# The expert layer of prompt tiles 1 to 3 as a dense pass over all 16,384 experts, tile 0 and the sample gathered

## The chip, the core and the metric

The kernel runs on one core of a Trainium2 chip. The metric is the device time in microseconds (us); the median of three runs of the kernel before is 4337.53 us (4334.4 to 4338.32).

## What is computed

One decoder layer for 512 prompt tokens and a sample group of 8 × 8 tokens, all in fp32, with a model width of 2048: norm and input projection, two parallel mixers (latent attention and gated linear attention), output projection, then an expert layer, then an embedding gated by a sigmoid. The expert layer is what the change is about. Each token has 8 heads; a head picks 16 of 16,384 experts by product keys, and each expert is one row of `peer_u` and one of `peer_v`:

```python
top_s, sel = lax.top_k(cand, PEER_TOPK)
e = jnp.take_along_axis(cidx, sel, -1)
gate = jax.nn.softmax(top_s.astype(F32), -1)
act = jax.nn.gelu(jnp.einsum("td,thkd->thk", xb, w["peer_u"][e]), approximate=False)
coef = (gate * act).astype(xb.dtype)
return jnp.einsum("thk,thkd->td", coef, w["peer_v"][e])
```

An expert's number is e = i1 × 128 + i2, where i1 and i2 are the picks among two lists of 128 keys.

## The kernel before, in words

Tokens lie in tiles of 128: tiles 0 to 3 are the prompt, tile 4 (`PT`) the 64 sample tokens. The front of the layer runs over `GROUPS` [0], [1, 2], [3, 4]: norm, input projection (`project`, L826; for group 1 it runs ahead, L1288), attention and linear attention (`mixer`), output projection, norm, queries (L1251), key scores. An fp32 matrix product is a sum over 16 slices of 128 of the contraction; SP loads each slab of 1 MB into one of four slots `W`. Then `best_keys` and `route` on VectorE pick the experts and make `idx_all` and `gate_all`.

A tile has 8 units, one for a head (the sample's 64 tokens are doubled onto 128 partitions and take 4). A unit is 16 gathers of `peer_u` rows, each 128 × 2048, a dot product for each (`dot_products`, L1968), a Gelu on ScalarE (L2485), then 16 gathers of `peer_v` rows and 16 weighted adds into `total` (`weighted_sum`, L1993). GpSimd issues the indirect DMAs (`gathers`, L2549) into a ring of 8 slots. 36 units make 576 gathers of either kind.

The order is written by hand. The front's work on VectorE is a generator, `woven`, cut into steps at its `yield`s. The main loop runs through the gathered rows; after each, `row_taken` runs the steps whose entry in `ROWS_BEFORE` is at most the number of rows taken. `STEPS_BEFORE` does the same on ScalarE for each unit's Gelu, `PAGES_BEFORE` on GpSimd for the cache pages of the sample attention. Each engine's queue is in order, so a step that waits holds what stands behind it. PE's program has only the front and the embedding, in order: groups 0, 1, 2, then `PLE_GROUPS` [0, 1], [2, 3], [4] (`project` and `embed`, L848; the sample's by `sample_embedding`). Before an embedding pass, the summed rows come back through `h2_dram`. The columns of `z` leave by `z_rows` on ScalarE (L2115), into the buffer that held the key scores, so the second half of group 2's projection waits for `best_keys` (L1589).

## Time and profile before

| | us |
|---|---|
| median of the runs | 4337.53 |
| profiled execution, span | 4331.6 |
| PE (TensorE matmul) busy | 2254.9, 52% |
| DVE (VectorE) busy | 3288.1, 76% |
| ACT (ScalarE) busy | 522.0, 12% |
| POOL (GpSimd) busy | 2201.2, 51% |
| DMA | 1599.51 MB, mean 369 GB/s |

Busy time is what the engine spends in instructions; issuing a DMA and waiting are not counted, except that the indirect DMAs of GpSimd are. PEld is the loading of PE's weights and overlaps PE. The granted clock is a share of TensorE's full speed, so 1.00 is 2.4 GHz and 0.5 is 1.2 GHz. The name behind an arrow is what ended the idle time before an instruction.

### The profile page before, as it was taken

What the parts mean: (1) busy time and instruction counts of PE and PEld (TensorE: products, weight loads), DVE (VectorE), ACT (ScalarE), POOL (GpSimd) and SP (SyncE); (2) the same over time, 40 slices, a digit from 0 to 9 for tenths busy, and PEclk for the clock granted to TensorE, in tenths of its full rate; (3) what the DMA queues carried; (4) which work ended last, traced back from release to release, by engine and by line L of the source; (5) the groups of instructions that cost most, each with busy time, mean ns of one, the idle gap of its engine ahead of it and who ended that gap; (6) DMA issues with size and microseconds to landing.
All of it is one profiled execution on the core that took longest, in us unless ns stands there. A gap on an engine that the chain in (4) does not pass through costs nothing.

```text
span 4331.6 us, 24058 instructions
## 1 busy us (share of the span) xinstructions
PE 2254.9 (52%) x8238; PEld 1342.1 (31%) x8238; DVE 3288.1 (76%) x3700; ACT 522.0 (12%) x1098; POOL 2201.2 (51%) x1216
## 2 busy tenths in 40 slices
PE   8999815425899492779942457710000920000755
PEld 4456403213475131367731222710000410000322
DVE  0130699997667998868889856699999699988673
ACT  2220112122002001212212010000001000001001
POOL 0000365744332556468775653345667368877441
PEclk9999956657999796767865678955555965555877
DMA  8658789988997999989999899988989999999996
GB/s 294 250 223 287 303 357 364 422 323 335 424 423 299 422 424 414 353 356 365 406 374 360 347 400 413 405 345 339 399 365 405 424 415 422 422 407 422 424 408 234
DMA packets 261153, 1599.51 MB, mean 369 GB/s; under 512 B 27763, under 2 KB 49459, under 8 KB 91750
## 3 DMA queue, kind: packets, MB, share of 16 engines
q0 software_dynamic: 176064, 1268.30, 72.0%
q1 hardware_dynamic: 83078, 320.64, 19.5%
q10 hardware_dynamic: 1888, 9.03, 0.5%
q8 instruction: 65, 1.06, 0.1%
q14 instruction: 58, 0.48, 0.0%
HBM read 1554.75 MB, written 42.56 MB: 369 GB/s over the span
## 4 chain that ended last, share of the span: by engine, by line
PE 31%; DVE 30%; POOL 16%; DMA 13%; issue 7%; ACT 2%; SPq 0%; DVEq 0%; ACTq 0%; POOLq 0%
POOL ring L2549 16%; PE bank L826 14%; DVE ring L1968 11%; DVE total L1993 9%; DMA ring<-in_peer_v,idx_all 5%; DMA ring<-in_peer_u,idx_all 5%; PE bank L1251 4%; PE bank L1288 3%; PE bank L929 1%; PE bank L891 1%; PE bank L800 1%; PE bank L1079 1%; DMA front<-in_cache_kv_latent,page_rows 1%; DVE front L1744 1%; PE bank L1093 1%
## 5 line engine op out<-in xcount | busy, mean ns | idle before, releaser
L1993 DVE SCALAR_TENSOR_TENSOR total<-ring,gate_all,total 128x2048 f32<-128x2048 f32 x571 | 1341.8, 2350 | 188.0 <-DMA ring<-in_peer_v,idx_all 164.5
L2549 POOL DMA_INDIRECT ring<-in_peer_u,idx_all x576 | 1062.2, 1844 | 795.7 <-DVE total L1993 359.1
L2549 POOL DMA_INDIRECT ring<-in_peer_v,idx_all x576 | 1072.2, 1861 | 711.9 <-DVE total L1993 376.3
L1968 DVE CUSTOM_DVE_ANT_0 ring<-ring,xrow 128x2048 f32<-128x2048 f32 x576 | 1297.5, 2287 | 169.4 <-DMA ring<-in_peer_u,idx_all 167.5
L826 PE MATMUL bank<-front 128*128 128x512 f32 (+3 forms) x1920 | 838.3, 594 | 68.9 <-ACT front L2115 64.6
L800 PE MATMUL bank<-inv_diag,front 128*128 128x128 f32 (+1 forms) x304 | 61.9, 391 | 1159.3 <-DVE inv_diag L1378 1102.2
L826 PEld LDWEIGHTS bank<-front 128*128 128x128 f32 (+1 forms) x1920 | 338.4, 181 | 558.5 <-issue 554.5
L800 PEld LDWEIGHTS bank<-inv_diag,front 128*128 128x128 f32 (+1 forms) x304 | 58.9, 299 | 1164.2 <-DVE inv_diag L1378 1098.2
L1251 PE MATMUL bank<-front 128*128 128x128 f32 (+2 forms) x1536 | 257.0, 329 | 20.5 <-DMA front<-in_peer_w_q 17.4
L1251 PEld LDWEIGHTS bank<-front 128*128 128x128 f32 x1536 | 239.8, 192 | 39.3 <-DMA front<-in_peer_w_q 20.3
L2574 POOL DMA_DIRECT2D ring<-in_w_in x12 | 10.7, 894 | 342.8 <-PE bank L1288 239.6
L1373 DVE RECIPROCAL st<-st 128x1 f32<-128x1 f32 (+1 forms) x20 | 3.2, 161 | 225.8 <-ACT st L2049 225.8
L1288 PE MATMUL bank<-ring 128*128 128x490 f32 x384 | 163.8, 574 | 2.1 <-ACT front L2115 2.1
L2485 ACT ACTIVATE dots<-dots 128x16 f32<-128x16 f32 x36 | 7.7, 215 | 804.2 <-DVE dots L1968 759.3
L913 PE MATMUL bank<-ident,front 128*128 128x128 f32 (+1 forms) x20 | 4.6, 380 | 170.9 <-DVE front L1426 99.4
L1288 PEld LDWEIGHTS bank<-ring 128*128 128x128 f32 x384 | 70.4, 190 | 74.7 <-issue 71.6
L1196 PE MATMUL bank<-front 128*128 128x128 f32 (+1 forms) x288 | 41.7, 314 | 93.0 <-DVE front L1695 81.9
L2501 POOL DMA_DIRECT2D xrow<-xn_dram x6 | 3.4, 573 | 163.1 <-DMA z_dram<-total 102.7
L1079 PE MATMUL bank<-ident,front 128*128 128x128 f32 x256 | 74.8, 395 | 7.4 <-DMA front<-in_cache_kv_latent,page_rows 5.8
L1575 DVE MAX8 front<-front 128x8 f32<-128x128 f32 (+1 forms) x80 | 19.2, 281 | 76.4 <-ACT front L2325 75.5
L1415 DVE TENSOR_TENSOR g_mla<-g_mla 128x128 f32<-128x128 f32 x1 | 0.3, 291 | 100.3 <-DMA g_mla<-in_qk_gain_q 100.3
L1119 PE MATMUL bank<-front 128*64 128x256 f32 x256 | 70.5, 444 | 6.9 <-ACT front L2357 6.9
(323 smaller groups left out, 2894.0 us busy)
## 6 DMA issues: line engine op xcount, KB each, us to landing
front<-in_w_in SPq DMA_DIRECT2D x64, 980.0 KB, 8.4
front<-in_w_out SPq DMA_DIRECT2D x48, 1024.0 KB, 9.1
front<-in_peer_w_q SPq DMA_DIRECT2D x48, 1024.0 KB, 13.3
front<-in_w_ple_gate SPq DMA_DIRECT2D x48, 1024.0 KB, 9.1
ring<-in_w_in POOLq DMA_DIRECT2D x12, 1960.0 KB, 10.5
front<-in_w_uq SPq DMA_DIRECT2D x6, 1536.0 KB, 10.7
ring<-in_peer_u,idx_all POOLq DMA_INDIRECT x576, 14.3
ring<-in_peer_v,idx_all POOLq DMA_INDIRECT x576, 16.0
```

The costliest lines, as they stand in the source:

```text
L800: mm = e.matmul(out, row, inv_diag[:R, :R], start=True, stop=True)
L826: mm = e.matmul(bank[4 * sl + c][:R, 0:ncol], XT[:, k, sl * P:sl * P + R], W[:, n % SLABS, c * ncol:(c + 1) * ncol], start=(k == 0), stop= ...
L891: mm = e.matmul(bank[c][:R, :], XT[:, k, 0:R], W[:, n % SLABS, c * BANK:(c + 1) * BANK], start=(k == 0), stop=False)
L929: mm = e.matmul(bank[j][:R, 0:2 * QK], cqT[:, slot(t), k, 0:R], wq[:, k, j * 2 * QK:(j + 1) * 2 * QK], start=(k == 0), stop=(k == 3))
L1079: e.transpose(bank[k][:, j * P:(j + 1) * P], latb[:, i, k * P:(k + 1) * P], ident[:, :])
L1093: mm = e.matmul(S, lt[0:ROPE, 2, j * P:(j + 1) * P], qrT[0:ROPE, b, :], start=False, stop=True)
L1119: e.matmul(bank[7][0:NS, 0:KVR], pTs[:, pg, :], latb[:, pg % HALF, :], start=(pg == 0), stop=False)
L1251: mm = e.matmul(bank[j][:, 0:ntok], W[:, n % SLABS, at:at + P], XT[:, k, 0:ntok], start=(k == 0), stop=(k == KD - 1))
L1288: mm = e.matmul(bank[6 + sl][:, 0:IN_BANK], xt[:, k, sl * P:(sl + 1) * P], chunk(n)[:, k % 8, :], start=(k == 0), stop=(k == KD - 1))
L1968: e.tensor_tensor_reduce(out=ring[:, b, :], in0=ring[:, b, :], in1=xrow[:, t % 2, :], scale=1.0, scalar=0.0, op0=ALU.mult, op1=ALU.add, ac ...
L1993: e.scalar_tensor_tensor(out=total, in0=ring[:, b, :], scalar=c1, in1=total, op0=ALU.mult, op1=ALU.add).then_inc(s("summed"), 1)
L2549: e.indirect_dma_start(out=ring[:, k % RING, :], out_offset=None, in_=a[("peer_u", "peer_v")[side]][0], in_offset=bass.IndirectOffsetOnAxi ...
```

## The change

Only tile 0 (8 units) and the sample (4 units) still gather. For tiles 1 to 3, 384 tokens (`ND`), every expert is computed:

- Two inputs are laid out anew on the host: `peer_u_t`, 128 tiles of 128 experts with the contraction on partitions, and `peer_v_t`, 32 blocks of 4 expert tiles, cut in four quarters of 512 columns.
- `route` keeps i1, i2 and the gate of each of a token's 128 picks in `picks` instead of making indices. `spread` turns them on PE (`picksT`), makes two one-hot matrices for each token on VectorE (128 picks × 128 keys, one of them times the gate), multiplies them on PE, which gives the 128 × 128 gates of the token, and stores these in `g_dram` through ScalarE's copies and DMA queue, 16 tokens at a time.
- PE turns the normed rows of the three tiles into `XD` (`turn_rows`). For each of 32 blocks (`NBLOCKS`) `expert_scores` makes 4 × 16 products of 384 columns, ScalarE applies Gelu into `CT`, VectorE multiplies by the block's gates (`weigh`), `expert_sums` makes 48 products of 512 columns (4 quarters × 3 tiles × 4 expert tiles) in 4 banks, and VectorE adds each of 12 sums to `acc` (`add_sums`). SP loads each megabyte into one of 5 buffers, two of them until the routes are done, and the block's gates in runs of 64 numbers.
- PE's order is now: groups 0 and 1, the projections of group 2, spreads 0 and 1, the mixer of group 2, `turn_rows`, scores of blocks 0 and 1, spread 2, then sums of b and scores of b + 2 in turn, then the embedding of all tiles in the groups [0], [1, 2], [3, 4].
- The ring has 5 slots. The three order tables are new: `STEPS_BEFORE` has 12 entries instead of 36, `ROWS_BEFORE` 1,207 instead of 705, with a last value of 384 gathered rows instead of 1,124. `h2_dram` and `sample_embedding` are gone; the embedding reads `h_dram` and adds `acc`. Some semaphores are shared.

The diff, cut to its core, without the tables:

```diff
-UNITS = PH * PT + PH // 2
-FIRST_UNITS = [t * PH for t in range(T)] + [UNITS]
+GATHERED, DENSE = [0, PT], [1, 2, 3]
+UNITS = PH + PH // 2
+FIRST_UNITS = {0: 0, PT: PH}
+UNITS_OF = {0: range(PH), PT: range(PH, UNITS)}
+XR = {0: 0, PT: 1}
 LAST = len(GROUPS) - 1
+ND = P * len(DENSE)
+ETILES = NKEY
+EB = 4
+NBLOCKS = ETILES // EB
+TURNS = 4 * len(DENSE)
+UNITS_V = 4 * len(DENSE)
+D_BUFS = 5
+FEW = 2
+FEW_LOADS = len(DENSE) + 3 * EB
+DENSE_LOADS = len(DENSE) + 2 * ETILES
+GROUP = 4
+CHUNK = 16
+G_GROUPS = P // GROUP
+G_CHUNKS = ND // CHUNK
+V_BANKS = [2, 3, 6, 7]
+LAST_DENSE = DENSE[-1]
...
+RING_SLOTS, RING = 8, 5
+STAGE = 6
+TILE_OF = [t for t in GATHERED for _ in UNITS_OF[t]]
...
+        XD = carve(KD, ND, at=0)
+        CT = [carve(EB, ND), carve(EB, ND)]
+        d_first = carve(D)
+        GB = [carve(G_CHUNKS, EB * CHUNK, at=h0 - 2 * EB * P), carve(G_CHUNKS, EB * CHUNK)]
+        d_bufs = [d_first, ring[:, RING, :]] + [carve(D, at=h0 + D), carve(D), carve(D)]
+        acc = [ring[:, STAGE, :], ring[:, STAGE + 1, :], carve(D, at=y0 + 2 * D + 4 * PLE)]
+        stage = [ring[:, STAGE + i, :].rearrange("p (i n) -> p i n", n=CHUNK) for i in range(2)]
+        onehot = xrow[:, XR[PT], :].rearrange("p (b w n k) -> p b w n k", b=2, w=2, n=GROUP)
...
+            def turned_rows():
+                e.wait_ge(s("xn_stored"), 16 * T)
+                e.wait_ge(s("slabs_used"), PASSES["gate0"])
+                for i, t in enumerate(DENSE):
+                    n = load_of("x", 0, i)
+                    d_free(e, n)
+                    e.dma_start(d_bufs[d_buf(n)], xn_dram[rows(t), :]).then_inc(d_sem(n), 16)
+            def expert_columns(b):
+                for i in range(EB):
+                    n = load_of("u", b, i)
+                    d_free(e, n)
+                    e.dma_start(d_bufs[d_buf(n)], a["peer_u_t"][EB * b + i]).then_inc(d_sem(n), 16)
+            def expert_rows(b):
+                for i in range(EB):
+                    n = load_of("v", b, i)
+                    d_free(e, n)
+                    if n >= FEW_LOADS:
+                        e.wait_ge(s("route_ready"), len(ROUTES))
+                    e.dma_start(d_bufs[d_buf(n)], a["peer_v_t"][b, i]).then_inc(d_sem(n), 16)
+            def gates(b):
+                if b >= 2:
+                    e.wait_ge(s("c_ready"), b - 1)
+                else:
+                    e.wait_ge(s("topk_done"), PH * (LAST_DENSE + 1))
+                    for i in range(2):
+                        e.wait_ge(s(f"g_stored{i}"), 16 * G_CHUNKS // 2)
+                e.dma_start(GB[b % 2], g_dram[:, :, EB * b:EB * (b + 1), :].rearrange("c p i n -> p c (i n)"))\
+                    .then_inc(s(f"pair_landed{b % 2}"), 16)
...
+            turned_rows()
+            expert_columns(0)
+            expert_columns(1)
...
+            for b in range(NBLOCKS):
+                gates(b)
+                if b >= 2:
+                    expert_columns(b)
+                if b >= 1:
+                    expert_rows(b - 1)
+            expert_rows(NBLOCKS - 1)
...
+            def spread(j):
+                e.wait_ge(s("picks_ready"), j + 1)
+                for w in range(3):
+                    mm = e.transpose(bank[7][:, w * P:(w + 1) * P], picks[:, w, :], ident[:, :])
+                mm.then_inc(s("picksT_psum"), 1)
+                for q in range(G_GROUPS):
+                    n = j * G_GROUPS + q
+                    e.wait_ge(s("onehot_ready"), n + 1)
+                    if n >= 2:
+                        e.wait_ge(s("g_staged"), n - 1)
+                    for i in range(GROUP):
+                        mm = e.matmul(bank[4 + n % 2][:, i * P:(i + 1) * P], onehot[:, n % 2, 1, i, :], onehot[:, n % 2, 0, i, :],
+                                      start=True, stop=True)
+                    mm.then_inc(s("g_psum"), 1)
+                    yield
+                e.wait_ge(s("g_staged"), (j + 1) * G_GROUPS)
+            def turn_rows():
+                e.wait_ge(s("scores_sb"), 4 * T)
+                for i in range(len(DENSE)):
+                    n = load_of("x", 0, i)
+                    e.wait_ge(d_sem(n), d_landed(n))
+                    for q in range(4):
+                        m = 4 * i + q
+                        if m >= 2:
+                            e.wait_ge(s("dense_sb"), m - 1)
+                        for j in range(4):
+                            k = 4 * q + j
+                            mm = e.transpose(bank[m % 2][:, j * P:(j + 1) * P], d_bufs[d_buf(n)][:, k * P:(k + 1) * P], ident[:, :])
+                        mm.then_inc(s("dense_psum"), 1)
+            def expert_scores(b):
+                for i in range(EB):
+                    n, m = load_of("u", b, i), TURNS + EB * b + i
+                    e.wait_ge(d_sem(n), d_landed(n))
+                    e.wait_ge(s("dense_sb"), max(m - 1, TURNS))
+                    for k in range(KD):
+                        mm = e.matmul(bank[m % 2][:, 0:ND], d_bufs[d_buf(n)][:, k * P:(k + 1) * P], XD[:, k, :],
+                                      start=(k == 0), stop=(k == KD - 1))
+                    mm.then_inc(s("dense_psum"), 1)
+            def expert_sums(b):
+                e.wait_ge(s("c_ready"), b + 1)
                 for c in range(4):
...
+                    n = load_of("v", b, c)
+                    e.wait_ge(d_sem(n), d_landed(n))
+                    for sl in range(len(DENSE)):
+                        u = UNITS_V * b + len(DENSE) * c + sl
+                        if u >= len(V_BANKS):
+                            e.wait_ge(s("v_added"), u - len(V_BANKS) + 1)
+                        for i in range(EB):
+                            mm = e.matmul(bank[V_BANKS[u % len(V_BANKS)]][:, :], CT[b % 2][:, i, sl * P:(sl + 1) * P],
+                                          d_bufs[d_buf(n)][:, i * BANK:(i + 1) * BANK], start=(i == 0), stop=(i == EB - 1))
+                        mm.then_inc(s("v_psum"), 1)
...
+                if g == LAST:
+                    for j in range(len(DENSE) - 1):
+                        now(spread(j))
...
+            turn_rows()
+            expert_scores(0)
+            expert_scores(1)
+            now(spread(len(DENSE) - 1))
+            for b in range(NBLOCKS):
+                expert_sums(b)
+                if b + 2 < NBLOCKS:
+                    expert_scores(b + 2)
...
+                if t in DENSE:
+                    if DENSE.index(t):
+                        e.wait_ge(s("picksT_psum"), DENSE.index(t))
+                    mark(e.tensor_copy(picks[:, 0, :], e1))
+                    mark(e.tensor_copy(picks[:, 1, :], e2))
+                    link(e.tensor_tensor(picks[:, 2, :].rearrange("p (h k) -> p h k", h=nh), g3,
+                                         gsum[:, 0:nh].unsqueeze(2).to_broadcast([P, nh, TOPK]), ALU.mult))
+                    e.sem_inc(s("picks_ready"), 1)
+                    e.sem_inc(s("route_ready"), 1)
+                    yield
+                    return
...
+            def spread(j):
+                yield
+                e.wait_ge(s("picksT_sb"), j + 1)
+                for q in range(G_GROUPS):
+                    n = j * G_GROUPS + q
+                    yield
+                    if n >= 2:
+                        e.wait_ge(s("g_psum"), n - 1)
+                    for i in range(GROUP):
+                        t = GROUP * q + i
+                        e.tensor_scalar(onehot[:, n % 2, 0, i, :], iota[:, :], picksT[:, 0, t:t + 1], picksT[:, 2, t:t + 1],
+                                        ALU.is_equal, ALU.mult)
+                        ins = e.tensor_scalar(onehot[:, n % 2, 1, i, :], iota[:, :], picksT[:, 1, t:t + 1], None, ALU.is_equal)
+                    ins.then_inc(s("onehot_ready"), 1)
+                yield
+            def weigh(b):
+                yield
+                e.wait_ge(s("dense_sb"), TURNS + EB * (b + 1))
+                e.wait_ge(s(f"pair_landed{b % 2}"), 16 * (H_GLA // 2 + b // 2 + 1))
+                ct = CT[b % 2].rearrange("p i (c n) -> p i c n", n=CHUNK)
+                e.tensor_tensor(ct, ct, GB[b % 2].rearrange("p c (i n) -> p i c n", i=EB), ALU.mult).then_inc(s("c_ready"), 1)
+            def add_sums(b):
+                for u in range(UNITS_V):
+                    n = UNITS_V * b + u
+                    yield
+                    e.wait_ge(s("v_psum"), n + 1)
+                    to = acc[u % len(DENSE)][:, u // len(DENSE) * BANK:(u // len(DENSE) + 1) * BANK]
+                    turned = bank[V_BANKS[n % len(V_BANKS)]][:, :]
+                    if b == 0:
+                        e.tensor_copy(to, turned).then_inc(s("v_added"), 1)
+                    else:
+                        e.tensor_tensor(to, to, turned, ALU.add).then_inc(s("v_added"), 1)
+            def experts():
+                yield from weigh(0)
+                for b in range(NBLOCKS):
+                    if b + 1 < NBLOCKS:
+                        yield from weigh(b + 1)
+                    yield from add_sums(b)
+                yield
...
+                    if t in DENSE:
+                        i = DENSE.index(t)
+                        e.wait_ge(s("rows_loaded"), ROWS_IN["ffn", LAST] + 16 * sum(x in DENSE for g in PLE_GROUPS[:pg + 1] for x in g))
+                        e.wait_ge(s("v_added"), UNITS_V * NBLOCKS + i)
+                        e.tensor_tensor(H[:, sl, :], H[:, sl, :], acc[i], ALU.add).then_inc(s("v_added"), 1)
...
+                yield from mixer(1)
+                yield from first_route(1)
+                yield from other_routes(1)
+                yield from spread(0)
+                yield from spread(1)
+                yield from mixer(2)
+                yield from best_keys(PT - 1, 0, PH)
+                yield from route(PT - 1, 0, PH)
+                yield from spread(2)
+                yield from best_keys(PT, 0, PH)
+                yield from route(PT, 0, PH)
+                yield from experts()
+                for pg in range(len(PLE_GROUPS)):
                     yield from embedding(pg)
             e.memset(eps[:, :], EPS).then_inc(s("fills_ready"), 1)
...
+                e.copy(picksT[:, :, :].rearrange("p w n -> p (w n)"), bank[7][:, 0:3 * P]).then_inc(s("picksT_sb"), 1)
+                per = CHUNK // GROUP
+                for q in range(G_GROUPS):
+                    n = j * G_GROUPS + q
+                    c, at = n // per, n % per * GROUP
+                    yield
+                    e.wait_ge(s("g_psum"), n + 1)
+                    if at == 0 and c >= 2:
+                        e.wait_ge(s(f"g_stored{c % 2}"), 16 * (c // 2))
+                    e.copy(stage[c % 2][:, :, at:at + GROUP].rearrange("p i n -> p n i"),
+                           bank[4 + n % 2][:, :].rearrange("p (n i) -> p n i", n=GROUP)).then_inc(s("g_staged"), 1)
+                    if at == CHUNK - GROUP:
+                        e.wait_ge(s("g_staged"), n + 1)
+                        e.dma_start(g_dram[c], stage[c % 2]).then_inc(s(f"g_stored{c % 2}"), 16)
+                yield
...
+                    e.activation(CT[b % 2][:, i, :], bank[m % 2][:, 0:ND], ACT.Gelu).then_inc(s("dense_sb"), 1)
...
+    u = np.ascontiguousarray(np.asarray(inputs["peer_u"], np.float32)[0].reshape(NKEY, NKEY, KD, P).transpose(0, 3, 2, 1)).reshape(NKEY, P, D)
+    v = np.ascontiguousarray(np.asarray(inputs["peer_v"], np.float32)[0].reshape(NBLOCKS, EB, P, 4, BANK).transpose(0, 3, 2, 1, 4))\
+        .reshape(NBLOCKS, 4, P, EB * BANK)
+    for name, v in (("peer_u_t", u), ("peer_v_t", v)):
+        arrays[f"in_{name}"] = v
+        a[name] = nc.dram_tensor(f"in_{name}", v.shape, F32, kind="ExternalInput").ap()
```

## Rows read from the trace of the kernel before

**Rows 1.** The page, part 2: the span in 40 slices, busy tenths and granted clock.

```profile
PE   8999815425899492779942457710000920000755
...
DVE  0130699997667998868889856699999699988673
...
PEclk9999956657999796767865678955555965555877
```

**Rows 2.** The page, part 5: the two gather groups.

```profile
L1993 DVE SCALAR_TENSOR_TENSOR total<-ring,gate_all,total 128x2048 f32<-128x2048 f32 x571 | 1341.8, 2350 | 188.0 <-DMA ring<-in_peer_v,idx_all 164.5
...
L1968 DVE CUSTOM_DVE_ANT_0 ring<-ring,xrow 128x2048 f32<-128x2048 f32 x576 | 1297.5, 2287 | 169.4 <-DMA ring<-in_peer_u,idx_all 167.5
```

**Rows 3.** Windows: length, busy us (x) of PE, PEld, DVE, ACT, POOL; clock, DMA share, GB/s.

```profile
0.00:579.00 579.00, 504.86 (x1839) 284.22 (x1839) 166.73 (x420) 102.99 (x236) 65.67 (x53) 0.96 0.74 269
579.00:1040.00 461.00, 163.37 (x594) 107.08 (x594) 431.15 (x461) 94.61 (x180) 286.29 (x146) 0.62 0.90 364
1040.00:1325.00 285.00, 254.36 (x928) 171.83 (x928) 185.32 (x150) 39.78 (x90) 89.24 (x67) 0.94 0.99 410
1325.00:1662.00 337.00, 238.85 (x576) 92.72 (x576) 299.23 (x563) 29.10 (x72) 159.30 (x93) 0.84 0.96 394
1662.00:2537.00 875.00, 503.12 (x2451) 371.48 (x2451) 742.72 (x736) 153.30 (x282) 591.24 (x289) 0.66 0.93 371
2537.00:2831.00 294.00, 236.07 (x926) 148.29 (x927) 194.30 (x143) 30.38 (x82) 120.27 (x80) 0.91 1.00 409
2831.00:4332.00 1501.00, 354.23 (x927) 166.42 (x924) 1268.68 (x1233) 71.88 (x159) 889.14 (x489) 0.61 0.95 387
```

**Rows 4.** Windows, L1968 alone: the two mixing stages.

```profile
579.00:1040.00 461.00, 168.28 (x150) 0.62 0.90 364
...
1662.00:2537.00 875.00, 287.44 (x256) 0.66 0.93 371
```

**Rows 5.** Windows, L1993 alone: the same two stages.

```profile
579.00:1040.00 461.00, 159.80 (x69) 0.62 0.90 364
...
1662.00:2537.00 875.00, 312.12 (x133) 0.66 0.93 371
```

**Rows 6.** Timeline of PE, 84 to 175: start, length, line, shape, count.

```profile
84.99 52.88 PE L826 MATMUL bank<-front 128*128 128x490 f32 x128 [0.75 <-ACT front L2115]
...
163.83 5.32 PE L929 MATMUL bank<-front 128*128 128x384 f32 x16
```

**Rows 7.** A window in which PE is busy throughout, columns as in rows 3.

```profile
300.00:470.00 170.00, 169.21 (x831) 111.42 (x829) 19.32 (x72) 21.05 (x56) 0.88 (x1) 1.00 0.78 276
```

**Rows 8.** Timeline of ACT, 1420 to 1665: the wait between the two projections.

```profile
1522.21 1.98 ACT L2115 COPY front<-bank 128x490 f32<-128x490 f32 x4 [96.75 <-DVE front L1589]
```

**Rows 9.** Groups of DVE by form: count, busy, mean ns.

```profile
L1902 DVE TENSOR_TENSOR front<-front,bank 128x512 f32<-128x512 f32 x16 | 10.9, 680 | 3.7 <-PE bank L848 3.7
L1854 DVE TENSOR_TENSOR front<-front,iota 128x1536 f32<-128x1536 f32 x6 | 10.5, 1754 | 0.1
...
L1484 DVE TENSOR_SCALAR ms<-ms 128x1 f32<-128x1 f32 x32 | 4.9, 154 | 1.1
...
L1378 DVE TENSOR_SCALAR inv_diag<-ident,st 128x128 f32<-128x128 f32 x12 | 3.6, 298 | 0.4
```

**Rows 10.** DMA issues: count, KB each, median us to landing.

```profile
front<-in_w_out SPq DMA_DIRECT2D x48, 1024.0 KB, 9.1
...
front<-in_state_gla SPq DMA_DIRECT2D x4, 1024.0 KB, 21.4
```

**Rows 11.** Timeline of PE, the last two-tile embedding pass.

```profile
4036.75 110.14 PE L826 MATMUL bank<-front 128*128 128x512 f32 x256 [0.46 <-ACT front L2394]
4147.66 13.97 PE L848 MATMUL bank<-front 128*128 128x512 f32 x32 [0.78 <-ACT front L2417]
```

**Rows 12.** Timeline of SP around the same pass: its store, the next pass's first load.

```profile
4168.91 5.64 SPq L763 DMA_DIRECT2D out_y_p<-front  x2
4182.98 0.50 SPq L758 DMA_DIRECT2D front<-in_p_sample  x1
```

413 lines of the change are left out of this document (203 added, 210 removed), and 85 rows, old and new, of the table ROWS_BEFORE.

## The prediction

> **What bounds the kernel now.** I read the span in slices first [rows 1]. VectorE (DVE) is at 6 to 9 tenths from slice 5 on, while TensorE (PE) is full only in the first slices and in blocks later and is nearly silent in slices 28 and 29 and 33 to 36, at the lower of its two clocks (5 tenths, 1.2 GHz). Then the costliest groups [rows 2]: the two gather operations, one dot product and one weighted add per gathered expert row, hold DVE for 1297.5 + 1341.8 = 2639 of its 3288 us. Then the stages [rows 3]: after 2831 us PE has 354 us of work in 1501 us while DVE has 1269 us; up to there the mixer stages run at a clock of 0.62 (579 to 1040) and 0.66 (1662 to 2537), with gaps. So the end is set by a queue of 1,152 gather operations of 2.3 us, woven into the mixer's DVE work. PE has room, but how much decides this case: busy time times granted clock, summed over the seven windows, is 505×0.96 + 163×0.62 + 254×0.94 + 239×0.84 + 503×0.66 + 236×0.91 + 354×0.61 = 1789 us of PE at full clock, and the idle parts pull those clocks down, so it is at least that.
>
> **The price of one matmul.** The code's second input projection has 16 steps of 4 matmuls, 64 calls; the timeline shows 128 rows in 52.88 us [rows 6], so every fp32 matmul is two rows, and a call of 490 columns costs 0.826 us. One row of 384 columns starts each 5.15/16 = 0.322 us (the next line starts at 168.98 us; 5.32 us less the overlap of the last), so a call costs 0.644 us; 512 columns take 110.14/256 = 0.430 us a row, 0.860 a call [rows 6, 11]. The clock in such stretches is 1.00, 2.4 GHz [rows 7].
>
> **Added: the dense pass on PE.** Scores: 128 expert tiles × 16 calls of 384 columns, 10.3 us a tile. Sums: 32 blocks × 4 quarters × 3 token tiles × 4 calls of 512, 12 × 0.860 = 10.3 us a quarter. A block is 8 × 10.3 = 82.5 us, 32 of them 2640 us, all in one engine's queue and nothing beside it on PE. PE's floor rises to 1789 + 2640 = 4430 us, above the present span of 4331.6 us, before any gap is counted.
> What feeds it is light. Per block: 8 loads of 1 MB (9.1 us each to landing, [rows 10]), five buffers, one consumed in 10.3 us; the gates, 3,072 runs of 256 B. The nearest row for short runs is the state load, 1,024 runs of 1 KB in 21.4 us [rows 10]; three times that is 64 us, still under 82.5 us and double-buffered. DVE: one product of 1,536 elements, 1.75 us, 12 adds of 512 at 0.68 us, 8.2 us, and 5.3 of the sample's gathered rows, 12 us: 22 us of 82.5 [rows 9]. ScalarE (ACT): 4 Gelus of 384 columns, under 3 us. So I take 82.5 us; the upper end is 86 (a gap at each hand-over), the lower end 82.
> The page "DMA: Bandwidth & Descriptors", section Specifications, of the Trainium skill speaks against the gate loads: transfers under 512 B are below line rate. No row here shows 256 B runs by themselves; even at a tenth of line rate the 0.79 MB would take about 20 us as an estimate, and the sum stays as it is.
>
> **Added: the dense gates.** Three spreads of 32 groups. A group is 8 one-hot operations of 128 columns on DVE, 4 calls on PE, one copy on ACT, a DMA issue on ACT's queue every fourth. For the one-hot operation there is only the neighbour L1378, 298 ns alone, and 154 ns for one column [rows 9]; back to back I take 0.20 us, 1.6 us a group plus hand-over, 55 us a spread (bounds 40 and 85). Spreads 0 and 1 stand in PE's program between the projections and the mixer of the last group, so the mixer waits for both: +110 us. Spread 2 is below.
>
> **Removed: 24 of 36 gather units**, 768 gathered rows: 768 × 2.32 = 1782 us of DVE, 805 MB. Only part was on the path before 2831 us. I counted the weaving steps of each stage in the code and looked them up in the new table: mixer of group 1 now has 60 gather rows beside it (table 16 to 76), the last mixer 95 (140 to 235), and the sample's 128 rows fall in dense blocks 0 to 22. What falls away:
> - 0 to 579: five rows fewer, −11, so 568.
> - 579 to 1040, 461 us: rows now cost 168 + 160 = 328 us [rows 4, 5]; DVE's other work is 103 us, so the rest is dependency latency. 60 rows are 137 us. A row taken away gives back between 0 and its whole length; I take 0.6 (PE's clock and gaps say that the chain is about half of it): 461 − 0.6 × 191 = 346. End 914.
> - 1040 to 1325, 285 us, PE 254 busy: stays. End 1199.
> - 1325 to 1662: the second projection waited for the selection, 96.75 us of ACT's wait [rows 8], because gather rows and selection shared DVE. Without them the two projections run on: 22 + 105 + 3 + 105 + 2 = 237, then spreads 0 and 1, 110 + 5. End 1551 against 1662; the gain of the selection is eaten by the spreads.
> - 1662 to 2537, 875 us, rows 287 + 312 = 600 us, now 217: 875 − 0.6 × 383 = 645. End 2196 against 2537.
> - 2537 to 2831, 294 us: fewer DMA waits, 270. End 2466.
>
> **Moved: start of the dense pass.** PE reloads and turns the rows of tiles 1 to 3 (25 us, three loads moved to SP's queue), does scores of blocks 0 and 1 with only two buffers (83 us), then spread 2 (55 us). DVE then selects for the sample tile, 57 us (114 us of non-gather work for two tiles, 1325 to 1662 [rows 3 to 5] less the gathers), and takes its first gathered row, about 28 us with the spread and load of the row on SP's and POOL's queues, before it weighs block 0. First sums at 2466 + 25 + 83 + 4 + 55 + 60 + 28 = 2721. PE idles some 85 us of that. The rest is 32 sum halves and 30 score halves: 62 × 41.25 = 2557. End 5278.
>
> **Moved: the embedding.** All five tiles now follow the last add, where before most lay under gathers. A two-tile pass is 110 + 14 us of PE [rows 11], about 35 us of loads, squares and transposes ahead and 14 us of store behind (4168.91 to 4182.98, [rows 12], the wait of the next pass for the store): 171. The one-tile pass: 14 + 57 + 8 + 13 = 92. Together 92 + 171 + 170 = 433. End 5711; the four stores of the summed rows go. The medians lie 6 us above the profiled execution's 4331.6, so 5717, rounded to 5720.
>
> **Rivals.**
> A. The gathers were the whole of the mixer stages (a row gives back 1.0): −76 and −153 us, 5490. For it: DVE 431 of 461 busy [rows 3]. Against it: PE and ACT chains at half clock in between.
> B. They were none of it (0), or the woven order, fixed for other durations, makes PE wait: DVE waits for a gathered row inside the adds, ACT for dot products ahead of a Gelu, four banks buffer only 10 us. With 0 the time is +115 +230 = 6060; 10 us in 23 blocks are +230, 5950. For it: ACT waits for dots in queue order; against it: DVE has 60 us of 82.5 free.
> C. The other side, not slower: a matmul is streamed once where I count twice. The place is the dense pass, the price 41 us a block; 5720 − 1320 = 4400, and with A's −229 it is 4171, faster. It decides once a block is under about 39 us alone, or 46 with A. Against it: 64 calls in 52.88 us [rows 6].
> The page "FP8 and Floating Point Precision", section TensorE Precision Notes, of the Trainium skill gives true fp32 four passes through the array; by that rule, 512 columns at 2.4 GHz take 0.853 us, and the trace's 0.860 agrees.
> D. The pass doesn't stay at 2.4 GHz for 2.6 ms. The longest stretch that the trace has is some 470 us at 1.00 [rows 1, 7]; beyond it nothing is shown. If a tenth of the clock goes, +290, 6010.
>
> **How the numbers follow.** Forecast 0.68, A 0.10, B 0.12, C 0.01, D 0.05, the rest spread about. The forecast's own bounds: gather share 0.6 ± 0.25 is ∓145, spreads −45 to +90, blocks −15 to +110, tail ± 30; together about −150 and +160. The range reaches a little to A and B: 5540 to 5910. About 0.2% is what a measurement of this kernel can tell from no change. Faster 0.01 (C), within 0.2% 0.01, slower 0.98: this rests on the floor of 4430 us, not on the weaving.
>
> **What would show it.** The changed profile should have PE at 9 tenths with clock 1.00 in nearly half of the slices; 4,096 score rows of 384 columns and 3,072 sum rows of 512 at 0.32 and 0.43 us; a block every 82.5 us; DVE under 4 tenths there, DMA under 5. The last mixer's norm should come near 2196, the first sum near 2721, the last near 5278. Gaps of PE within blocks with a releaser on DVE or ACT would be B; mixer stages of 270 and 490 us A. A block of 41 us would prove the forecast wrong as a whole.

## The result, and the profile after

| | before | after |
|---|---|---|
| median, us | 4337.92 | 5759.47 (5752.01 to 5768.67) |
| ratio to before | | 1.328, 95% interval 1.326 to 1.330 |
| profiled execution, span, us | 4331.6 | 5764.9 |
| PE busy | 52% | 87% |
| DVE busy | 76% | 35% |
| DMA, MB | 1599.5 | 1105.6 |

The change makes the kernel 1421.6 us slower. Of the page of the changed kernel, these are the busy times, four lines of the 40 slices (PE, DVE, granted clock, DMA), the chain by engine, and the largest groups of the dense sums (L1063) and dense scores (L1048); those that read a buffer in `ring` stand in smaller groups of their own.

```profile
PE 5022.0 (87%) x16199; PEld 2808.4 (49%) x16199; DVE 2027.1 (35%) x3672; ACT 651.6 (11%) x1283; POOL 570.6 (10%) x438
...
PE   8996546889668965895699999999999999999789
...
DVE  0306676462873456336322222322232211111110
...
PEclk9998668999876776998899999999999999999999
DMA  8586658854455448642655555555555533332543
...
PE 82%; DVE 10%; DMA 3%; ACT 2%; issue 2%; SPq 0%; POOL 0%; DVEq 0%; ACTq 0%
...
L1063 PE MATMUL bank<-front 128*128 128x512 f32 x2424 | 1047.6, 592 | 0.0
L1048 PE MATMUL bank<-front 128*128 128x384 f32 x3200 | 1041.3, 487 | 5.0 <-DMA front<-in_peer_u_t 5.0
```

PE is at 9 tenths in all slices from 20 to 36 (counted from 0), with the clock at 9; before, PE was nearly silent in much of that half [rows 1]. DVE is at 1 to 3 tenths beneath it. 82% of the chain is PE. The windows by stage (length, busy us of PE, PEld, DVE, ACT, POOL with counts, clock, DMA share, GB/s) are group 1's mixer, spreads 0 and 1, the last mixer, its output and queries, the start of the dense pass, the dense pass, and the embedding:

```profile
573.00:918.00 345.00, 165.00 (x594) 108.69 (x594) 242.68 (x329) 90.41 (x176) 100.56 (x61) 0.64 0.62 231
1454.00:1603.00 149.00, 83.67 (x519) 71.59 (x519) 137.08 (x528) 73.41 (x82) 13.88 (x8) 0.87 0.52 202
1603.00:2277.00 674.00, 501.02 (x2451) 371.04 (x2452) 366.89 (x484) 138.40 (x265) 169.09 (x119) 0.71 0.57 211
2277.00:2535.00 258.00, 235.87 (x944) 150.60 (x944) 65.42 (x79) 31.42 (x85) 19.41 (x18) 0.94 0.64 241
2535.00:2786.00 251.00, 130.94 (x547) 87.17 (x547) 168.56 (x649) 46.46 (x55) 8.11 (x8) 0.80 0.32 112
2786.00:5352.00 2566.00, 2560.65 (x6912) 1314.68 (x6912) 599.64 (x607) 61.07 (x125) 127.11 (x124) 1.00 0.48 161
5352.00:5765.00 413.00, 350.36 (x891) 157.07 (x890) 41.65 (x56) 52.07 (x126) 0.00 (x0) 0.92 0.44 158
```

These answer to [rows 3]. The front of the layer ends at 2535 us instead of 2831, 296 us earlier, although the spreads take 145 us of it. Behind it stood 1501 us; now it is 3230, and 2566 of them are the sixth row, in which PE is idle for 5 us, at a clock of 1.00.

### The profile page after: what moved, and what is told of

Same layout as the page of the kernel before. It is cut to its first block, busy times and chain, and to the rows that moved or that the text cites. A ratio compares the mean times of both kernels' runs of the same rounds, so it can differ in the third digit from the quotient of the medians.

```text
span 5764.9 us, 39836 instructions
## 1 busy us (share of the span) xinstructions
PE 5022.0 (87%) x16199; PEld 2808.4 (49%) x16199; DVE 2027.1 (35%) x3672; ACT 651.6 (11%) x1283; POOL 570.6 (10%) x438
## 4 chain that ended last, share of the span: by engine, by line
PE 82%; DVE 10%; DMA 3%; ACT 2%; issue 2%; SPq 0%; POOL 0%; DVEq 0%; ACTq 0%
PE bank L1063 23%; PE bank L1048 23%; PE bank L979 16%; PE bank L1414 4%; PE bank L1451 3%; DVE xrow L2079 2%; DVE xrow L2081 1%; PE bank L953 1%; PE bank L1282 1%; PE bank L1092 1%; PE bank L1256 1%; PE bank L1242 1%; DVE total L2244 1%; PE bank L1254 1%; DVE ring L2219 1%
## 5 line engine op out<-in xcount | busy, mean ns | idle before, releaser
L1063 PE MATMUL bank<-front 128*128 128x512 f32 x2424 | 1047.6, 592 | 0.0
L1048 PE MATMUL bank<-front 128*128 128x384 f32 x3200 | 1041.3, 487 | 5.0 <-DMA front<-in_peer_u_t 5.0
L1048 PEld LDWEIGHTS bank<-front 128*128 128x128 f32 x3200 | 608.7, 190 | 435.3 <-issue 12.5
L1063 PEld LDWEIGHTS bank<-front 128*128 128x128 f32 x2424 | 460.6, 190 | 574.6 <-issue 568.0
L2244 DVE SCALAR_TENSOR_TENSOR total<-ring,gate_all,total 128x2048 f32<-128x2048 f32 x190 | 446.4, 2350 | 80.9 <-DMA ring<-in_peer_v,idx_all 77.9
L2219 DVE CUSTOM_DVE_ANT_0 ring<-ring,xrow 128x2048 f32<-128x2048 f32 x192 | 436.7, 2286 | 96.4 <-DMA ring<-in_peer_u,idx_all 95.6
L2825 POOL DMA_INDIRECT ring<-in_peer_v,idx_all x192 | 259.6, 1352 | 1688.3 <-DVE total L2244 1237.9
L2825 POOL DMA_INDIRECT ring<-in_peer_u,idx_all x192 | 262.2, 1366 | 1362.2 <-DVE dots L2219 1094.0
L1063 PE MATMUL bank<-ring,front 128*128 128x512 f32 x648 | 284.5, 595 | 90.7 <-DMA ring<-in_peer_v_t 90.7
L1048 PE MATMUL bank<-front,ring 128*128 128x384 f32 x896 | 297.6, 491 | 5.5 <-ACT front L2663 4.8
L1414 PEld LDWEIGHTS bank<-front 128*128 128x128 f32 x1536 | 240.6, 192 | 18.4 <-issue 3.6
L1063 PEld LDWEIGHTS bank<-ring,front 128*128 128x128 f32 x648 | 123.8, 191 | 245.2 <-issue 243.6
L1048 PEld LDWEIGHTS bank<-front,ring 128*128 128x128 f32 x896 | 172.0, 192 | 128.0 <-issue 13.1
```

Source lines behind the costliest of these rows:

```text
L1048: mm = e.matmul(bank[m % 2][:, 0:ND], d_bufs[d_buf(n)][:, k * P:(k + 1) * P], XD[:, k, :], start=(k == 0), stop=(k == KD - 1))
L1063: mm = e.matmul(bank[V_BANKS[u % len(V_BANKS)]][:, :], CT[b % 2][:, i, sl * P:(sl + 1) * P], d_bufs[d_buf(n)][:, i * BANK:(i + 1) * BANK], ...
L1414: mm = e.matmul(bank[j][:, 0:ntok], W[:, n % SLABS, at:at + P], XT[:, k, 0:ntok], start=(k == 0), stop=(k == KD - 1))
L2219: e.tensor_tensor_reduce(out=ring[:, b, :], in0=ring[:, b, :], in1=xrow[:, XR[t], :], scale=1.0, scalar=0.0, op0=ALU.mult, op1=ALU.add, ac ...
L2244: e.scalar_tensor_tensor(out=total, in0=ring[:, b, :], scalar=c1, in1=total, op0=ALU.mult, op1=ALU.add).then_inc(s("summed"), 1)
L2825: e.indirect_dma_start(out=ring[:, n % RING, :], out_offset=None, in_=a[("peer_u", "peer_v")[side]][0], in_offset=bass.IndirectOffsetOnAxi ...
```

## What was expected and what came

The ends of the changed kernel's stages beside the predicted ones, in us; the last column is the miss of that stage alone:

| end of | predicted | measured | miss of the stage |
|---|---|---|---|
| first stage | 568 | 573.5 | +5.5 |
| mixer of group 1 | 914 | 918.3 | −1 |
| output, queries of group 1 | 1199 | 1200 | −3 |
| projections of group 2 | 1436 | 1457.8 | +21 |
| spreads 0 and 1 | 1551 | 1603.0 | +30 |
| last mixer | 2196 | 2277.0 | +29 |
| its output and queries | 2466 | 2535 | −12 |
| start of the sums | 2721 | 2786.4 | −4 |
| last sum | 5278 | 5352 | +9 |
| last store | 5711 | 5765 | −20 |

## Experiments

A time without an interval is that of a single run. A kernel's line numbers can lie a few above those of the changed kernel.

**1. Half of the dense products.**

```diff
-                    for k in range(KD):
-                        mm = e.matmul(bank[m % 2][:, 0:ND], ...
+                    for k in range(KD // 2):
+                        mm = e.matmul(bank[m % 2][:, 0:ND], ...
...
-                        for i in range(EB):
+                        for i in range(EB // 2):
                             mm = e.matmul(bank[V_BANKS[u % len(V_BANKS)]][:, :], ...
```

> Leaves out half of the dense products: a score sums 8 of its 16 slices of the contraction, a sum takes 2 of its 4 expert tiles; loads, gates, Gelus, weighing and adds stay. Theory (the count of PE's matmul rows at 2.4 GHz sets the dense pass, everything else has room): a block falls from 82.5 to 41.3 us, so the 2566 us from the first sum to the last become about 1283 and the time 5759 - 1283 = 4476 us. Rival (the feed is the next limit): the same 427 MB must come in 1283 us, 333 GB/s as a mean and about 356 in the blocks with gathered rows, against 161 now; if they come at 300 GB/s, blocks take 48 us and the time is about 4650. Rival of the adds: VectorE needs 22 us of a block and would not show.

Measured: 4469.4 us. Windows of it, in the blocks with gathered rows, and from the first sum to the last:

```profile
2840.00:3340.00 500.00, 500.00 (x1362) 258.36 (x1361) 257.31 (x260) 24.70 (x52) 66.74 (x67) 1.00 0.98 364
2753.00:4062.00 1309.00, 1290.35 (x3472) 662.53 (x3473) 578.22 (x610) 65.74 (x133) 128.65 (x124) 0.99 0.88 316
```

The dense pass took 1309 us for the expected 1283; the difference lies in its first 87 us, where two loads came 14 us late and the clock was at 0.88. PE has no idle time in the first of these windows although DMA is at 0.98 of its time and moves 364 GB/s. So the count of matmul rows sets the pass, and halving the rows halves it: 5759.5 − 4469.4 = 1290 us for 16 of 32 blocks' worth, 40.3 us a half block. Even at this half price, with half of the products left out, the single run is 3% slower than the kernel before.

**2. A quarter of the feed.**

```diff
-                    e.dma_start(d_bufs[d_buf(n)], a["peer_u_t"][EB * b + i]).then_inc(d_sem(n), 16)
+                    e.dma_start(d_bufs[d_buf(n)][:, 0:D // 4], a["peer_u_t"][EB * b + i][:, 0:D // 4]).then_inc(d_sem(n), 16)
```

and the same for `peer_v_t`.

> Leaves out three quarters of each load of an expert tile (512 of 2048 columns are loaded; the products run over old numbers). Theory (loads are fully hidden behind PE): the dense pass keeps 2566 us; only the first sum comes a few us earlier; 5745 to 5765 us. Rival (loads slow PE's or VectorE's access, or end small waits at hand-overs): 1 us a block or more, 5730 or less.

Measured: 5754.0 us, ratio to before 1.326 (1.324 to 1.329), not to be told from the changed kernel's. A window of its dense pass, columns as above:

```profile
2786.00:5338.00 2552.00, 2548.38 (x6889) 1309.46 (x6888) 596.15 (x605) 61.19 (x125) 127.45 (x124) 1.00 0.28 85
```

85 GB/s instead of 161, and PE as busy as before; from the first sum to the last it takes 2563.5 us instead of 2565.2. Three quarters of the loads, with whatever contention they bring, are worth nothing in the fp32 pass. The hand-overs between engines stay in this run; what they can cost is bounded by PE's 5 us of idle time in the changed kernel. Together with experiment 1 this closes the dense pass: its price is its matmul rows.

**3 and 4. What tile 0's gathered rows cost the mixers.** First only their work on DVE, then the gathers altogether.

```diff
+                    w = P if t == 0 else D
-                    e.tensor_tensor_reduce(out=ring[:, b, :], in0=ring[:, b, :], in1=xrow[:, XR[t], :], ...
+                    e.tensor_tensor_reduce(out=ring[:, b, 0:w], in0=ring[:, b, 0:w], in1=xrow[:, XR[t], 0:w], ...
```

> Leaves out 15 of 16 columns of tile 0's dot products and weighted adds on VectorE (128 of 2048); its gathers and all waits stay. It asks what a gathered row costs a mixer stage. Theory (by parts of the stage: where PE is at 9 tenths, as in the sample attention, a row costs 0.15 of its length; in the linear attention 0.87; in the latent attention 0.3): the last mixer has 224 us of such work and falls from 704 by about 80 to some 625 us; the mixer of group 1 (136 us of such work) from 345 to about 275; the time is about 5605. Rival (0.6 everywhere, as predicted): 704 - 117 = 587, 5570. Rival (whole): 704 - 195 = 509, 5446. Rival (nothing): 5759. The dense pass keeps 2566 us in all of them.

```diff
+                    if t in SKIP:
+                        e.memset(dots[:, XR[t], i:i + 1], 0.5).then_inc(s("dots_done"), 1)
+                        row_taken()
+                        continue
```

with `SKIP` = [0], the same for the weighted adds, and no indirect DMA for these rows.

> Leaves out the gathers of tile 0 altogether: no indirect DMA, and each dot product and weighted add of tile 0 is one fill of a single column, with the same order of steps. The run with thin rows fell by 59 us only, because VectorE then waited 369 us for the rows' DMAs instead. Theory (by parts of the stage; a removed row gives back 0.15 in the sample attention, where PE is at 9 tenths, 0.3 in the latent attention, 0.87 in the linear attention, all of it in the tail): the last mixer falls from 704 to about 610, that of group 1 from 345 to about 275; with 25 us at the spreads, where six gathered adds are left, the time is about 5575. Rival (what is left of the mixers is their own chain of dependent steps and hides rows of tile 0 wholly): last mixer 660 as with thin rows, 5700. Rival (0.6 everywhere): 570 and 263, 5525.

Measured: 5700.8 us with thin rows, where 5605 was expected, and 5625.9 us with none, where 5575 was. The expectations took the last mixer from the wrong point: 704 us counts the last 30 us of the spreads in; it is 674, from PE's first transpose at 1603.0 (below) to the norm at 2277.0. By that measure it falls to 634 with thin rows (1575.9 to 2210.4) and to 627 with none (1509.8 to 2136.8); group 1's mixer from 345 to 337 and 280; the spreads from 135 to 122 and 120 us, first matmul to last. The two gather groups of DVE in the mixers and spreads, first in the changed kernel (573 to 2277 us):

```profile
L2219 DVE CUSTOM_DVE_ANT_0 ring<-ring,xrow 128x2048 f32<-128x2048 f32 x112 | 254.6, 2287 | 59.9 <-DMA ring<-in_peer_u,idx_all 59.3 <-DVE front L1914 0.4 <-DVE front L1723 0.2
L2244 DVE SCALAR_TENSOR_TENSOR total<-ring,gate_all,total 128x2048 f32<-128x2048 f32 x106 | 249.3, 2352 | 45.5 <-DMA ring<-in_peer_v,idx_all 42.9 <-DVE front L1723 0.2
```

then in the thin one (573 to 2211 us):

```profile
L2246 DVE SCALAR_TENSOR_TENSOR total<-ring,gate_all,total 128x128 f32<-128x128 f32 x106 | 37.1, 350 | 107.4 <-DMA ring<-in_peer_v,idx_all 105.3 <-DVE front L1723 0.2
L2220 DVE CUSTOM_DVE_ANT_0 ring<-ring,xrow 128x128 f32<-128x128 f32 x112 | 30.7, 286 | 132.6 <-DMA ring<-in_peer_u,idx_all 132.0 <-DVE front L1914 0.4 <-DVE front L1723 0.2
```

DVE's work on these rows has fallen from 504 to 68 us, but the wait for the rows to land (the number after the second bar) has grown from 105 us to 240. Only 59 us of the kernel's time came back with the work; another 75 came back when the gathers went too. So a gathered row in DVE's in-order queue is priced by its landing as well as by the operation on it. The expectation missed this: all three theories priced only DVE's work.

With the rows gone the prices by part come out. Three parts of the last mixer, latent attention, sample attention and linear attention, first before (columns as above):

```profile
1662.00:1868.00 206.00, 97.32 (x301) 50.36 (x301) 192.30 (x199) 41.82 (x81) 133.31 (x67) 0.64 0.95 376
1934.00:2224.00 290.00, 262.56 (x1517) 208.43 (x1517) 251.63 (x214) 52.62 (x102) 235.42 (x111) 0.78 0.93 377
2224.00:2486.00 262.00, 81.23 (x332) 57.38 (x330) 237.34 (x278) 38.88 (x65) 162.65 (x77) 0.60 0.94 367
```

then in the changed kernel:

```profile
1603.00:1751.00 148.00, 95.34 (x301) 48.18 (x301) 98.71 (x140) 37.63 (x77) 42.39 (x31) 0.71 0.64 237
1821.00:2090.00 269.00, 260.72 (x1516) 207.95 (x1516) 112.59 (x120) 50.22 (x98) 61.73 (x48) 0.80 0.49 179
2090.00:2240.00 150.00, 77.83 (x333) 55.14 (x331) 108.58 (x187) 33.22 (x59) 37.80 (x22) 0.67 0.60 212
```

and without tile 0's rows:

```profile
1510.00:1638.00 128.00, 92.13 (x301) 46.12 (x300) 39.24 (x126) 37.58 (x77) 4.80 (x5) 0.74 0.22 80
1704.00:1972.00 268.00, 261.39 (x1513) 207.99 (x1513) 44.48 (x103) 50.22 (x98) 14.98 (x16) 0.79 0.16 58
1972.00:2118.00 146.00, 80.25 (x334) 57.67 (x334) 59.62 (x169) 33.20 (x59) 0.56 (x1) 0.67 0.27 87
```

| part | before: gather work, length | after | no rows |
|---|---|---|---|
| latent attention | 157, 206.0 | 62, 148.1 | 0, 128.3 |
| its preparation for the sample | 30, 66.3 | 14, 70.2 | 0, 66.0 |
| sample attention | 213, 289.2 | 71, 268.4 | 0, 267.8 |
| linear attention | 179, 262.1 | 50, 149.9 | 0, 146.0 |
| tail | 21, 51.4 | 22, 37.4 | 0, 18.9 |
| sum | 600, 875 | 219, 674 | 0, 627 |

The lengths are read between PE's first instructions of each part (the tail begins with PE's last matmul of the linear attention), the gather work from L1968 and L1993 (L2219 and L2244 after) alone. In the sample attention PE is busy 263 of 290 us before and 261 of 268 without any row: it is bound by PE, and 213 us of gather work cost it 21. In the linear attention PE works only 81 of 262 us; there the first 129 us of removed work gave back 112, the last 50 gave back 4. So the share is no property of a row: it was 0.87 where DVE had hardly any idle time (linear attention, DVE busy 237 of 262 us) and 0.15 where PE had hardly any (sample attention, 21 of 142 us). It also falls as rows go, and the name of the busiest engine doesn't tell it: after the change DVE is still the busiest one of the linear attention (109 of 150 us, PE 78), yet its last 50 us gave back 4, while the 22 us of the tail, in which PE has nothing to do, gave back 18.5. The predicted 0.6 was right for group 1's mixer (345 us, predicted 346), whose remaining 136 us of rows then gave back 65, and a little high for the last mixer (201 of 381 us removed, 0.53), as a mean over parts as different as these.

**5. The sums' earlier start.**

```diff
                 yield from spread(2)
+                yield from weigh(0)
+                yield from weigh(1)
+                yield from add_sums(0)
                 yield from best_keys(PT, 0, PH)
```

with `gates`, `expert_rows(0)` and `expert_columns(2)` ahead of the sample's spread on SP, and `expert_gelus(2)` ahead of the route on ACT.

> The same computation. After spread 2 VectorE weighs blocks 0 and 1 and adds the sums of block 0 before it selects for the sample tile (tile 3's part waits in the buffer total, since its own place is still used by the selection), SP loads the gates and the rows of block 0 and the columns of block 2 ahead of the sample's spread, ScalarE does the Gelus of block 2 first. Theory (PE's 91 us of idle time before the first sum are the selection of the sample, its spread and first gathered row, all of which can lie beside sums of block 0 and scores of block 2): what stays is the load of the gates, some 25 to 35 us; 5759 - 60 = about 5700 us. Rival (the gates of block 0, in runs of 256 B, land late, some 60 us after the last spread): the gain is 20 us or less, 5740. Rival (the selection moves on and PE waits for it later, before the sums of block 1): 5750.

Measured: 5732.7 us (1.321, 1.319 to 1.323), 27 us less, not 60. In the changed kernel PE's timeline has one wait here:

```profile
2786.39 12.47 PE L1063 MATMUL bank<-ring,front 128*128 128x512 f32 x24 [90.66 <-DMA ring<-in_peer_v_t]
```

In this one it has three (first sum, then sums of block 1):

```profile
2699.04 6.53 PE L1066 MATMUL bank<-ring,front 128*128 128x512 f32 x8 [17.07 <-DMA ring<-in_peer_v_t]
...
2821.44 11.95 PE L1066 MATMUL bank<-front 128*128 128x512 f32 x24 [36.81 <-issue]
...
2851.10 9.05 PE L1066 MATMUL bank<-ring,front 128*128 128x512 f32 x16 [14.28 <-DVE ring L2109]
```

The gates were quicker than expected: 17 us from the last spread to the first sum, where 25 to 35 were named. But the selection of the sample now stands behind block 0's adds, and by SP's program the loads of `peer_v_t` for block 1 come after its end (36.8 us of PE; the row names no releaser); then DVE takes the sample's first dot products, which wait for their rows (15.3 us for the first), before it weighs and adds again (14.3 us of PE). The three waits together are 68 of the 91 us: the rival was right that the wait moves on, the theory that part of it is gone.

**6. The kernel before without the gathers of tiles 1 to 3.** The edit is that of experiment 4 with `SKIP` = [1, 2, 3].

> The kernel before, without the gathers of tiles 1 to 3 (no indirect DMA, each dot product and weighted add a fill of a single column) and without the dense pass: it leaves out the expert layer of these tiles. It asks what the gathers of the three tiles were worth on the path, 1782 us of VectorE's work. Theory (stages as in the changed kernel, without its spreads: ends at 573, 918, 1200, 1454, 2158, 2416; then 114 us of selection for two tiles, 28 to the first gathered row, 128 rows of 2.33 us, 90 us of the last embedding): about 2950 us, so the gathers held 1390 us of the path, 0.78 of their work. Rival (the gathers were the whole of it): 4338 - 1782 = 2556. Rival (half of them lay in gaps): 3450.

Measured: 3274.8 us. Windows of group 1's mixer, of the last mixer, its output and queries, and of the rest:

```profile
580.00:1043.00 463.00, 167.23 (x594) 108.84 (x594) 430.90 (x461) 94.83 (x180) 280.99 (x145) 0.61 0.90 363
1602.00:2231.00 629.00, 488.83 (x2452) 364.88 (x2453) 164.78 (x611) 153.84 (x282) 24.29 (x27) 0.74 0.23 82
2231.00:2487.00 256.00, 232.91 (x928) 147.98 (x928) 14.16 (x127) 30.98 (x83) 0.00 (x0) 0.93 0.45 146
2487.00:3273.00 786.00, 355.81 (x922) 166.06 (x922) 458.12 (x1039) 71.43 (x158) 229.31 (x137) 0.72 0.67 265
```

The theory had 2950. So the three tiles' gathers held 4338.9 − 3274.8 = 1064 us of the path, 0.60 of their 1782 us. The theory missed by 325 us, at three places above all. Group 1's mixer stays at 463 us (345 expected), since all of its rows are tile 0's: in the changed kernel it got shorter only because the new table puts fewer of them there. The last mixer takes 629 us (704 expected, in which the end of the spreads was counted), as it does without tile 0's rows above, so 628 is its own length. And the rest takes 786 us instead of 530: the table, made for other durations, puts the embedding's steps, in which DVE waits 121 us for PE's products of one pass, between the sample's rows. So 1064 us is the price of the gathers with this order of steps left as it was; an order made for the kernel without them could only make it larger. Against the same kernel the dense way to these three tiles costs 5759.5 − 3274.8 = 2485 us; the matmuls alone are 2640 us of PE in it.

**7 and 8. One row per matmul.** ScalarE rounds every loaded megabyte to bf16.

```diff
+                    e.wait_ge(d_sem(m), d_landed(m))
+                    if m - H_BUFS >= len(DENSE):
+                        used_by_pe(e, m - H_BUFS)
+                    e.copy(h_bufs[m % H_BUFS], d_bufs[d_buf(m)]).then_inc(s("keysT_sb"), 1)
...
-                        mm = e.matmul(bank[m % 2][:, 0:ND], d_bufs[d_buf(n)][:, k * P:(k + 1) * P], XD[:, k, :],
+                        mm = e.matmul(bank[m % 2][:, 0:ND], h_bufs[n % H_BUFS][:, k * P:(k + 1) * P], XD[:, k, :],
```

`XD` and `CT` are bf16 too, and `keysT_sb`, a semaphore that was free by then, counts the rounded loads.

> Changes the arithmetic of the dense pass: ScalarE rounds each loaded megabyte, the turned rows and the Gelus to bf16, the gate product is bf16, and the sums are fp32 in the banks; everything else stays fp32. Theory (each matmul is then one row at 1 column a cycle, so PE needs 64 x 0.16 + 48 x 0.215 = 20.6 us a block, a quarter of 82.5, and the feed becomes the bound: 9.2 MB a block, with the gathered rows of blocks 0 to 22 some 14.9 MB, at the 420 GB/s that the trace shows at best, 36 and 22 us a block): the dense pass takes about 1020 us instead of 2566, the time is about 4210 us. Rival (ScalarE, with eight copies of 1.9 us and its turns with PE in one queue, or VectorE's adds, add up instead of overlapping): 45 us a block, 4630. Rival (bf16 matmuls cost as much as fp32's): 5760.

> The bf16 arithmetic of the dense pass as in the other kernel, and with it the earlier start of the sums (block 0's weighing and sums and block 2's scores ahead of the sample's selection). Theory: the start of the sums is worth the same 27 us as it was alone, or less, since the blocks that fill the idle time are four times as short: the other kernel less 10 to 27 us, about 4190. Rival (the order delays the sample's gathered rows, which with short blocks are the last to finish): slower than the other kernel by up to 20 us.

Measured: 4210.5 us, ratio to before 0.970 (0.969 to 0.972), and with the earlier start 4214.5 us, 0.972 (0.970 to 0.973). Of the first one's page, the busy times, the slices of PE and DMA, and the groups of the sums, the rounding and the scores:

```profile
PE 3148.1 (75%) x12583; PEld 1796.0 (43%) x12615; DVE 1998.3 (47%) x3672; ACT 1124.0 (27%) x1539; POOL 579.9 (14%) x438
...
PE   8999917449889856799755995166676666887979
...
DMA  8758666678954447535559643399999999996333
...
L1071 PE MATMUL bank<-front 128*128 128x512 bf16 x1504 | 410.7, 427 | 310.5 <-ACT front L2673 131.0
...
L2673 ACT CAST front<-front 128x2048 bf16<-128x2048 f32 x201 | 381.5, 1898 | 422.2 <-DMA front<-in_peer_u_t 278.7
...
L1056 PE MATMUL bank<-front 128*128 128x384 bf16 x2048 | 368.1, 339 | 118.7 <-ACT front L2673 62.5
```

The scores are 2,048 rows in a kernel that had 4,096 of them, for the same 2,048 calls: bf16 is one row a call where fp32 is two. PE is at 6 to 8 tenths in slices 26 to 35 (from 0), and DMA at 9 in each of these. Windows in the blocks with gathered rows, and in the last few:

```profile
2770.00:3560.00 790.00, 530.33 (x2321) 231.47 (x2340) 441.66 (x444) 351.48 (x256) 116.93 (x116) 0.88 1.03 396
3680.00:3805.00 125.00, 110.90 (x570) 54.82 (x573) 55.16 (x77) 87.77 (x63) 0.00 (x0) 1.00 0.96 358
```

In the first window DMA is at its full time (1.03 by the records) with 396 GB/s, and PE is busy 530 of 790 us: the bound has moved from PE to the transfers, as the 36 us a block said (37.8 from one block's weighing to the next). In the last blocks, 24.0 us each for an expected 22, PE is busy 111 of 125 us, so there the transfers do not bind alone. The sums run from 2747 to 3802, 1055 us for an expected 1020. The earlier start is of no use here: the two kernels' intervals overlap. Blocks a quarter as long don't fill the selection (PE waits 65.9 and 21.3 us there). The sample's gathered rows begin 27 us later, as the rival had it, but their last ones end at the same time (3594 and 3596 us), so the slowdown that it named is not shown either. The kernel before computes this layer in fp32 throughout; these two round its operands, so they are not the same arithmetic.

**9. Gates in long runs.** The last window above moves 358 GB/s where the expert rows alone could come at 420.

```diff
-        g_dram = scratch("g_dram", G_CHUNKS, P, NKEY, CHUNK)
+        g_dram = scratch("g_dram", NBLOCKS, P, G_CHUNKS, EB * CHUNK)
...
-                        e.dma_start(g_dram[c], stage[c % 2])
+                        e.dma_start(g_dram[:, :, c, :].rearrange("b p x -> p b x"), stage[c % 2].rearrange("p (b i) n -> p b (i n)", i=EB))
...
-                e.dma_start(GB[b % 2], g_dram[:, :, EB * b:EB * (b + 1), :].rearrange("c p i n -> p c (i n)"))\
+                e.dma_start(GB[b % 2], g_dram[b])\
```

> The bf16 kernel with the gates laid out in memory by block instead of by chunk of 16 tokens: the 98,304 runs of 256 B are then in ScalarE's 24 stores during the spreads, and a block's gates are read in runs of 6 KB. Theory (the dense pass in bf16 is bound by DMA time and the short runs take more of it than their bytes: blocks 23 to 31 move 9.2 MB at 358 GB/s, 25.6 us, where their 8.4 MB of expert rows at 420 GB/s would be 20 us, so the gates cost 5.6 us a block and would cost 1.9 in long runs): 3.7 x 32 = 118 us less in the dense pass; a store of 4,096 short runs takes about 7.5 us against a chunk every 7.24 us in the spreads, so up to 10 us more for each of three spreads. 4210 - 118 + 20 = about 4110 us. Rival (the runs cost the same by bytes, or the wait for the rows of tile order sets the blocks): 4210. Rival (stores in short runs hold the spreads, 11 us a chunk): 24 x 3.6 = 86 us back, 4180.

Measured: 4149.1 us, ratio to before 0.957 (0.955 to 0.958). It is the fastest of all, 188 us under the kernel before. The sums run from 2735 to 3736, 55 us less than with short runs and not 118. From one block's weighing to the next it is 35.6 us instead of 37.8 in blocks 2 to 22, and 21.8 instead of 24.0 in the last seven: 2.2 us a block where 3.7 were expected. In the last blocks little more could come, since PE is busy 86 of the 90 us from 3570 to 3660. The window from which the 3.7 were read was thus one in which PE bound nearly as much as the transfers. Spreads 0 and 1 took the same 135 us with the short runs in their stores; DMA was at 0.75 of its time there, at 0.56 in experiment 7.

## Why the prediction was right, point by point

5720 was predicted and 5759.5 measured, inside the range of 5540 to 5910, and slower as forecast. The mechanism came as described. That the last store misses by only 54 us is partly luck: the stages that were forecast too short add up to 95 us, those forecast too long to 40.

- **The floor.** PE's 4430 us was the argument, and it carries the result: the new page has 5022 us of PE busy in a span of 5765.
- **The block.** 82.5 us from two rows a matmul. The timeline in the last blocks, four score tiles and then quarters of sums:

```profile
5228.39 41.44 PE L1048 MATMUL bank<-front 128*128 128x384 f32 x128
5269.66 10.46 PE L1063 MATMUL bank<-ring,front 128*128 128x512 f32 x24
5279.97 41.36 PE L1063 MATMUL bank<-front 128*128 128x512 f32 x96
5321.16 10.46 PE L1063 MATMUL bank<-ring,front 128*128 128x512 f32 x24
```

41.3 us from the first row to the second is four score tiles, 10.3 a quarter of sums, 41.2 four of them. From the first sum to the end of the last one it is 2565.6 against 2557 us. The two feeds that were only bounded were far below their bounds: the gates land in 8.1 us where 64 were allowed, the expert tiles in 4.9 where [rows 10] gave 9.1 (count, KB, median us to landing):

```profile
front<-in_peer_v_t SPq DMA_DIRECT2D x24, 1024.0 KB, 4.8
front<-in_peer_u_t SPq DMA_DIRECT2D x22, 1024.0 KB, 4.9
...
front<-g_dram SPq DMA_DIRECT2D x6, 768.0 KB, 8.1
```

DVE was busy 600 us, 19 of 82.5 a block (predicted 22). The Trainium skill, page "DMA: Bandwidth & Descriptors", section Specifications, puts transfers below 512 B under line rate. The trace agrees: 0.79 MB in 8.1 us is 97 GB/s, where 1.05 MB in long runs takes 4.9 us, 214 GB/s; and experiment 9 shows its price once DMA is the bound.
- **The clock.** 1.00 over 2566 us: rival D's ground was only that nothing so long had been shown.
- **Rivals A and B's first half**, a share of 1.0 or of 0 for the rows taken out of the mixers, fell by the stages: 345 and 674 us, where A named 270 and 490 and a share of 0 would have left 461 and 875.
- **Rival C**, the other side, fell by its row count, and by experiment 1: with a block at 41.3 us the time was 4469, where the working gave 4400. It was the right rival to write down: experiment 7 makes it true by another arithmetic, and then the kernel is faster.
- **Rival B's second half**, PE waiting within blocks, did not come: 5 us in 2566. Two score banks and four sum banks were enough, with DVE idle for three quarters of each block. One sign was set too low: DMA is at 5 tenths in slices 20 to 31, where under 5 was named.
- **The spreads** were mis-sized: 110 + 5 us predicted, 145 measured. The first transpose, the first matmuls, the worst wait, the last two groups, and the first transpose of the mixer:

```profile
1457.76 0.90 PE L1012 MATMUL bank<-ident,picks 128*128 128x128 f32 x3 [4.42 <-ACT front L2355]
1461.53 3.89 PE L1020 MATMUL bank<-xrow 128*128 128x128 f32 x16 [2.87 <-DVE xrow L2081]
...
1493.13 3.76 PE L1020 MATMUL bank<-xrow 128*128 128x128 f32 x16 [10.09 <-DVE xrow L2081]
...
1593.76 1.16 PE L1020 MATMUL bank<-xrow 128*128 128x128 f32 x8 [0.65 <-DVE xrow L2081]
1595.57 1.16 PE L1020 MATMUL bank<-xrow 128*128 128x128 f32 x8 [0.65 <-DVE xrow L2081]
1602.99 1.09 PE L1076 MATMUL bank<-ident,front 128*128 128x128 f32 x4 [6.26 <-issue]
```

A group is 1.81 us, not 1.72: a pair of one-hot operations starts every 0.45 us, where 0.20 was taken for each of the two. That is 116 us for 64 groups. Between the first matmul and the last lie 135 us; of the other 19, fifteen are the price of six gathered adds woven between the groups, during which PE stands still (without tile 0's rows the same stretch is 120 us), to which the prediction gave none. Another 3.8 us pass ahead of the first group and 6.3 between the last one and the mixer.
- **The projections of group 2** took 258 us, not 237: two of 112 instead of 105 us, and 28 instead of 22 in front. The 105 were twice the 52.88 us of [rows 6], from the first stage; the trace of the kernel before has 112.6 and 113.1 us for these two projections themselves (from 1346.5 and from 1522.9 us). Why a row is dearer here than there stays open.
- **The last mixer** took 674 us, not 645; the share is the term that failed, 0.53 for 0.6, for the reason in experiments 3 and 4.
- **The first stage** did not gain its 11 us with five rows fewer: 573.5; without any rows it is 568.0.
- **The start of the sums** (251 us from 2535, predicted 255) and its cause, the selection ahead of the weighing, came as worked out, with one wait of 90.7 us where 85 were named (the sum there has 60 us for a selection that it works out as 57). **The tail** took 413 us, predicted 433: the second pass starts 101 us after the first, the third 163 after the second, where 113 and 171 were worked out.
- **The medians**: 6 us were added for the distance between span and median. In this kernel the median lies 5 us below the profiled span. The two errors of this kind and the misses of the table, +54 us at the last store, leave the 39.5 us.

## What to carry to other kernels

A move of work from a busy engine to an idle one is priced first by the floor of the new engine: all that it has to do, at its best rate. PE's 1789 us and the 2640 us of added fp32 matmuls make 4430 us, more than the 4338 us of the whole kernel before, and this settles the sign before any overlap is looked at. The gathers that went held 1782 us of DVE and 1064 us of the time. Computing 16,384 experts for 384 tokens did not pay at half of the fp32 price (4469 us, with half of the products left out) and did at a quarter of it, in bf16 (0.957 of before, at bf16's rounding); then the transfers become the bound, and their run lengths matter. The share of a removed piece of work that comes back must be read part by part, from how little idle time the engine that does it has in that part, and for a gather the landing counts beside the arithmetic.

## What the runs showed of the hardware

- PE held the granted clock at 1.00, 2.4 GHz, through 2566 us of fp32 matmuls without a gap over 5 us.
- With DMA at 0.98 of its time and 364 GB/s, PE was busy 500.00 of 500 us (experiment 1).
- In bf16 (last blocks of experiment 9), 64 rows of 384 columns took 10.56 us, 0.165 us each, half of the fp32 row's 0.322: with half the rows the call is a quarter of the price.
- The two one-hot operations on 128 columns last 0.34 us (two operands of one value per partition) and 0.28 us (one such operand); the next one starts 0.26 and 0.20 us after them.
- A store of 1 MB in 4,096 runs of 256 B every 7.2 us added nothing to the 135 us of spreads 0 and 1 (experiment 9); the stores landed in 6.2 us (median), in long runs in 3.9 (experiment 7).
